# Two half quarters ahead of the first scores, a block sum split later, three gate buffers, a wait per block at the join, gate tiles ahead of weights

## What is computed

```
h = rms_norm(x, g_mix); z = h @ w_in
q, k, v, r, a_lr, c_b, c_c, c_x, g_a, g_b = split_columns(z)
o = gla_chunked(q, k, v, log_sigmoid(a_lr @ w_alpha_up + b_alpha) / 16)   # 4 heads, chunks of 64
o = rms_norm(o, g_gla) * silu(r)
y_a = o @ w_branch_a
y_b = (c_b * causal_dwconv(c_c * c_x, w_conv)) @ w_branch_b
x = x + (sigmoid(g_a) * y_a + sigmoid(g_b) * y_b) @ w_out
```

## Time and profile before

| | |
|---|---|
| time, median of 3 runs | 2441.77 us (2439.71 to 2442.86) |
| the profiled execution: its own time | 2438.01 us |
| its span, first to last instruction | 2436.4 us |
| PE busy | 2367.5 us (97%) |
| DVE busy | 1669.9 us (69%) |
| ACT busy | 1271.2 us (52%) |
| POOL busy | 384.8 us (16%) |
| mean granted TensorE clock | 0.989 of full speed |

### The profile page before, as it was taken

How to read it: one execution, slowest core, us unless ns; L and a number is a source line. 1 busy time by engine, 2 the same in 40 slices (tenths; PEclk the granted TensorE clock), 3 DMA queues, 4 the chain that set the end, 5 groups by cost and what they waited for, 6 DMA issues and landing times.

```text
span 2436.4 us, 40291 instructions
## 1 busy us (share of the span) xinstructions
PE 2367.5 (97%) x13303; PEld 1877.5 (77%) x13304; DVE 1669.9 (69%) x1750; ACT 1271.2 (52%) x1348; POOL 384.8 (16%) x412
## 2 busy tenths in 40 slices
PE   7999999999999999978999999999999999999996
PEld 7887777878887887876788777777777787777775
DVE  5212556757667264276789887888877998788977
ACT  5413653232223021165677665767666776667766
POOL 0000000000000001452121212122122121212120
PEclk9999999999999999998999999999999999999998
DMA  5133234353444333457999898989889998989998
GB/s 136 35 46 54 61 95 96 82 78 70 71 76 156 130 121 123 154 187 258 332 376 379 304 333 291 375 307 379 303 315 309 385 378 282 336 307 378 346 341 305
DMA packets 264906, 553.77 MB, mean 227 GB/s; under 512 B 29464, under 2 KB 76312, under 8 KB 263712
## 3 DMA queue, kind: packets, MB, share of 16 engines
q1 hardware_dynamic: 241536, 497.74, 61.0%
q0 software_dynamic: 23296, 55.03, 8.0%
HBM read 501.70 MB, written 51.02 MB: 227 GB/s over the span
## 4 chain that ended last, share of the span: by engine, by line
PE 53%; DVE 1%; issue 0%; ACT 0%; DMA 0%; POOLq 0%; DVEq 0%; ACTq 0%
PE m_y L2610 5%; PE m_gate L2612 5%; PE m_gate L2610 5%; PE m_lin L2610 5%; PE m_lin L2612 5%; PE m_gate L2611 5%; PE m_lin L2611 5%; PE m_y L2612 5%; PE m_y L2611 5%; PE m_spill L2649 4%; PE m_spill L2661 2%; PE m_turn L2594 1%; PE m_gate L2618 1%; PE m_y L2618 1%; PE m_lin L2618 1%; PE m_lin L2580 1%
## 5 line engine op out<-in xcount | busy, mean ns | idle before, releaser
L2418 DVE TENSOR_TENSOR m_w_lo<-raw,m_w_hi 128x2048 fp32r<-128x2048 f32 x382 | 867.1, 2288 | 204.4 <-ACT m_w_hi L2293 198.5
L2293 ACT CAST m_w_hi<-raw 128x2048 fp32r<-128x2048 f32 x382 | 730.9, 1914 | 351.3 <-PE m_lin L2612 236.8
L121 PE MATMUL c_bank<-h_hi_r,ring_hi 128*128 128x512 f32 x656 | 259.7, 396 | 3.4 <-DVE qk_r L1341 2.1
L2610 PE MATMUL m_gate<-m_w_hi,x_hi 128*128 128x512 f32 x508 | 216.2, 426 | 0.0
L2610 PE MATMUL m_y<-m_w_hi,m_a_hi 128*128 128x512 f32 x512 | 210.3, 411 | 1.8 <-DVE m_a_lo L2470 1.8
L2612 PE MATMUL m_y<-m_w_hi,m_a_lo 128*128 128x512 f32 x512 | 199.9, 390 | 0.0
L2611 PE MATMUL m_y<-m_w_lo,m_a_hi 128*128 128x512 f32 x512 | 199.8, 390 | 0.0
L2612 PE MATMUL m_gate<-m_w_hi,x_lo 128*128 128x512 f32 x508 | 199.2, 392 | 0.0
L2611 PE MATMUL m_gate<-m_w_lo,x_hi 128*128 128x512 f32 x508 | 198.6, 391 | 0.0
L2610 PE MATMUL m_lin<-m_w_hi,x_hi 128*128 128x512 f32 x508 | 198.6, 391 | 0.0
L2612 PE MATMUL m_lin<-m_w_hi,x_lo 128*128 128x512 f32 x508 | 198.3, 390 | 0.0
(11 more groups left out here) (416 smaller groups left out, 4675.2 us busy)
## 6 DMA issues: line engine op xcount, KB each, us to landing
raw<-in_w_gate_up SPq DMA_DIRECT2D x512, 512.0 KB, 11.1
raw<-in_w_down SPq DMA_DIRECT2D x256, 512.0 KB, 14.6
ring_raw<-in_w_in SPq DMA_DIRECT2D x31, 1024.0 KB, 9.6
gates<-work POOLq DMA_DIRECT2D x32, 256.0 KB, 3.8
work<-gates SPq DMA_DIRECT2D x8, 1024.0 KB, 7.2
v<-in_x SPq DMA_DIRECT2D x8, 512.0 KB, 6.0
r_rows<-work POOLq DMA_DIRECT2D x16, 256.0 KB, 2.8
o_rows<-v SPq DMA_DIRECT2D x8, 512.0 KB, 11.1
```

What stands on the lines that cost most here:

```text
L121: pe.matmul(out, left_hi(k), right_hi(k), start=first and k == kts[0], stop=False, skip_group_check=True)
L2293: act.copy(w_hi[:, p % WS].rearrange("p k b n -> p (k b n)"), raw[:, raw_slot(m)].rearrange("p k b n -> p (k b n)")).then_inc(signals.whi, 1)
L2418: dve.tensor_tensor(w_lo[:, p % WS].rearrange("p k b n -> p (k b n)"), raw[:, raw_slot(m)].rearrange("p k b n -> p (k b n)"), f32(w_hi[:, ...
L2610: pe.matmul(out, left_hi[:, kt], right_hi, start=False, stop=False, skip_group_check=True)
```

## The change

Five edits:

1. In the first attention tile, `gate_product(1, 0)` (12 matmuls) stands ahead of `score(0)` instead of between `update(0)` and `output(0)`.
2. ACT's `form_high(2)`, `form_high(3)` and `turned_hi(3)` stand ahead of the last `light_out` of the plain gate panels; DVE's `turned_lo(3)` moves from ahead of the seven-product loop to z = 0, f = 2.
3. A third gate buffer, and a semaphore for each buffer: `light_out(k)` waits for the store of quarter k-3. The new buffer lies over a buffer of the r gate, so quarter 2 also waits for the r gate's stores.
4. At the end of the projections PE waits before each of the four k blocks for that block's b_lo, not for all five b_lo at once.
5. In the join, SP loads the weights of panel A+1 only when silu tiles 5, 6 and 7 have landed.

```diff
@@ buffers
-        stream = take(2, HALF)
+        stream = [take(HALF), take(HALF)]
...
+        stream.append(take(HALF))
+        STREAMS = len(stream)
@@ stores
-        def gate_stores(k):
-            return 16 * (GATES // 2 + k // 2)
+        def stores(s, k=STREAMED):
+            return 16 * len(range(s, k, STREAMS))
@@ light_out, on ACT
-                if k >= 2:
-                    act.wait_ge(gate_stored[k % 2], gate_stores(k))
-                act.activation(stream[:, k % 2], value, ACT.Sigmoid).then_inc(light_done, 1)
+                if k >= STREAMS:
+                    act.wait_ge(stream_stored[k % STREAMS], stores(k % STREAMS, k))
+                if k == 2:
+                    for s in range(2):
+                        act.wait_ge(gate_stored[s], 16 * GATES // 2)
+                act.activation(stream[k % STREAMS], value, ACT.Sigmoid).then_inc(light_done, 1)
@@ plain gate panels, on ACT
                 act.wait_ge(ready, results(n) + r + 1)
+                if k == 4 * LIGHTS - 1:
+                    form_high(2)
+                    form_high(3)
+                    turned_hi(3)
                 light_out(k, banks[4 * (n % 2) + r][:, :])
...
-            form_high(2)
-            form_high(3)
-            turned_hi(3)
@@ DVE
             form_low(3)
-            turned_lo(3)
...
                     for at_m in forms_at(z, f):
                         form_low(at_m)
+                    if z == 0 and f == 2:
+                        turned_lo(3)
@@ PE, attention
             for i in range(TT):
                 gate_product(2 * i, 0)
+                if i == 0:
+                    gate_product(1, 0)
                 score(i)
                 gate_product(2 * i, 1)
                 update(i)
-                gate_product(2 * i + 1, 0)
+                if i:
+                    gate_product(2 * i + 1, 0)
                 output(i)
                 gate_product(2 * i + 1, 1)
@@ PE, end of the projections
-            pe.wait_ge(b_lo_done, HEADS + 1)
             pe.wait_ge(light_done, STREAMED)
             for k in range(HEADS):
+                pe.wait_ge(b_lo_done, k + 2)
                 for j in range(4):
                     channel_product(pe, ring, END, banks[j][:, :], b_hi, b_lo, j, kts=[k], first=k == 0, last=False)
@@ SP, join
                 sp.wait_ge(ready, results(n - 1))
+                if n == A + 1:
+                    for s in range(2, EARLY):
+                        sp.wait_ge(silu_loaded[s], 16)
```

More of the change, by code:

```diff
@@ L670, in attend_and_project @@
         gate_done, gate_stored = sem("gate_done"), signals.gate_stored
+        stream_stored = signals.stream_stored
         ready = sem("ready")
@@ L745, in _ @@
                 pool.wait_ge(light_done, k + 1)
-                pool.dma_start(gates[:, n * BPP + r // 2, (r % 2) * HALF:(r % 2 + 1) * HALF], stream[:, k % 2]) \
-                    .then_inc(gate_stored[k % 2], 16)
+                pool.dma_start(gates[:, n * BPP + r // 2, (r % 2) * HALF:(r % 2 + 1) * HALF], stream[k % STREAMS]) \
+                    .then_inc(stream_stored[k % STREAMS], 16)
             for s in range(2):
-                pool.wait_ge(gate_stored[s], gate_stores(STREAMED))
+                pool.wait_ge(gate_stored[s], 16 * GATES // 2)
+            for s in range(STREAMS):
+                pool.wait_ge(stream_stored[s], stores(s))
         @block.scalar
@@ L869, in _ @@
                     if z == SEVENS - 1 and f == 2:
-                        for s in range(2):
-                            act.wait_ge(gate_stored[s], gate_stores(STREAMED))
+                        for s in range(STREAMS):
+                            act.wait_ge(stream_stored[s], stores(s))
                         act.copy(b_hi(HEADS), qk[:, HEADS]).then_inc(b_hi_done, 1)
@@ L2007, in __init__ @@
         self.gate_stored = [sem(f"gate_stored{s}") for s in range(2)]
+        self.stream_stored = [sem(f"stream_stored{s}") for s in range(3)]
         self.added = [sem(f"added{x}") for x in range(2)]
```

## The result

The changed kernel takes 2428.0 us (median of 5 runs, 2424.68 to 2432.04), beside 2441.77 for the kernel before (5 runs, 2439.71 to 2448.45): a ratio of 0.9941, with a 95% interval of 0.9921 to 0.9961. It is faster by 0.6%, or 13.8 us in the medians; 10.5 were forecast, for a time of 2431.3. The profiled execution took 2432.04 us with a span of 2430.4, the slowest of the five.

What follows compares the result with a forecast made beforehand. PE, busy 97% of the span, bounds the kernel, so only its gaps and slow clock can give: 4.5 + 1.2 + 1.3 + 2.4 + 1.1 = 10.5 us off 2441.8 gives 2431.3 us, range 2427.5 to 2436.0.

Steps and rivals of the forecast that it cites:

- no stall for the states: First attention tile: DVE's states stay 0.2 us ahead of the outputs; stall costed at nothing, 0.5 us at most.
- The rival, that the clock falls in tile 0 all the same: First attention tile: PE's clock still falls, gain 8.8 us instead of 10.5, time 2433.0 us; chance 0.11.
- The barrier's 0.3 us of room: Join's barrier: DVE's last split ends at 783.49, 0.3 us before PE now arrives at 783.8; it barely fits.
- the part on the clock: Attention stage: clock 0.50 behind the 3.04 us gap, full speed behind shorter ones; filling it gains 4.5 us, otherwise 2.85.
- the 3.8 us by which the profiled execution lay under the median: Whole kernel: profiled execution took 2438.0 us, 3.8 under the median; 10.5 was subtracted from the median 2441.8.
- The router rival: Router stage: 12 us more PE work at the lower clock gives back 6 us, time 2437.3 us; chance 0.11.
- a sign of being wrong: Listed signs: new gaps before first outputs, product 5 of z = 0, the barrier or panel A+1; or a longer router stage.
- The weights of A+1: Panel A+1: held weights land 6.2 us late at worst loads, gain falls to 3.2 us, time 2438.6; slower-case chance 0.03.

Runs made afterwards that it cites:

- before, second: The kernel before plus a register operation holding the expert stage's loaded routed-row counts at zero or above: 2439.64 us (11 runs), 0.9999 to the original.
- before, third: The kernel before with the same register operation on the expert stage's counts, run once more: 2442.07 us in one run.
- after, second: The changed kernel plus a register operation holding the expert stage's loaded counts at zero or above, against the kernel before with it: 2429.22 us (6 runs), 0.9954.
- after, third: The changed kernel with the same register operation, timed once more against the kernel before: 2426.74 us (5 runs), 0.9944.
- the second series: Both kernels again, each with only a register operation on the expert stage's counts added: before 2439.64 us, changed 2429.22 us, ratio 0.9954.
- The two kernels built on the change: The changed kernel with panel A's last two tiles' transposes moved ahead (2428.28 us, 0.9935 to before), and with the join's single b_lo wait restored (2434.21 us, 0.9958).

## Why the prediction was right, and where it fell short

The stretch piece by piece, in three profiles of each kernel (each figure the difference of two starts on PE: first scores, fourth product of z = 0, that of z = 5, first product behind the join's barrier, first of the output stage; the total begins at the stage's start, 6.0 us ahead of the scores):

| profile | scores to z = 0 | to z = 5 | to the barrier | to the output stage | total |
|---|---|---|---|---|---|
| before | 208.09 | 97.87 | 253.76 | 175.50 | 741.24 |
| before, second | 208.12 | 97.90 | 259.06 | 175.11 | 746.21 |
| before, third | 208.13 | 97.94 | 256.79 | 175.15 | 744.05 |
| after | 202.72 | 96.28 | 250.93 | 174.31 | 730.27 |
| after, second | 202.71 | 96.39 | 251.41 | 174.33 | 730.87 |
| after, third | 202.72 | 96.40 | 253.56 | 174.32 | 733.03 |
| forecast gain | 5.7 | 1.3 | 2.4 | 1.1 | 10.5 |
| mean gain | 5.4 | 1.5 | 4.6 | 0.9 | 12.4 |

- **Edit 1**, 4.5 counted, 4.3 measured alone (208.09 - 203.78). Scores at the old time, full clock behind them, no stall for the states: all as said. The rival, that the clock falls in tile 0 all the same, is refuted in each of the seven profiles that have the whole or half block ahead. The Trainium skill ("TensorE: Matmul & The Clock Gate", section "What's actually happening") has the throttled state as the default that activity releases; the trace agrees, since filling 2.7 of the 3.04 us kept the clock at 1.00.
- **Edit 2**, 1.2 counted, 1.1 measured. `turned_lo(3)` stood from 432.63 to 434.9 and held up no product.
- **Edit 3**, 1.3 counted, 1.5 measured up to z = 5: that gap went to 0.69 to 1.03 where 1.0 was said. The reason given, that quarter 15 still waits for the store of quarter 12, is what the trace shows. What the sum did not have is z = 12, which stands behind gate panel z = 11 as z = 5 stands behind z = 4, and had no gap in the one profile that I read. In the eight profiles with two buffers it is 0.93 us on average, from nothing to 1.93; in the six with three buffers 0.50, from nothing to 2.33. It hangs on a store's landing in both, and with this scatter no gain there is shown.
- **Edit 4**, 2.4 counted, 2.5 measured alone. From z = 5 to the barrier the changed kernel against the one with three buffers alone gives the same, 253.46 - 250.93 = 2.5. The barrier's 0.3 us of room held: the split ends at 777.65 and the product starts at 778.18, with the same 0.30 before it as ever.
- **Edit 5**, 1.1 counted, 0.8 to 1.2 measured. Silu tiles 5 to 7 loaded in 3.8 to 5.5 us in all six profiles with this edit, no wait of DVE for a silu tile in panel A, and DVE bound by PE's transposes as said, which moving them ahead then proved. The rule of the Trainium skill weighed for it ("DMA: Bandwidth & Descriptors", section "Queues, rings and completion order"), that an engine takes packets in turn from its queues, agrees for the silus: without the weights beside them the last one lands in 5.3 us and not in 10.3. Its other use, that a third store does not slow the two ahead of it, agrees too: the store of quarter 12 (gate panel z = 4) landed after 11.6, 11.6 and 11.5 us in the three profiles of before and after 11.5, 11.7 and 11.7 in those of after, and the one behind it after 9.6 to 9.8 in all six.

The fixed parts measured add up to 4.3 + 1.1 + 1.5 + 2.5 + 0.9 = 10.3 us, 10.5 counted. **The step that failed** is the one in the part on the clock, that "the first matmuls behind the gaps of 1.36, 1.87 and 2.23 us are drawn at 0.47 to 0.50 us, as at full speed", read as if the clock did not fall behind these gaps, so that each was priced at its length and 0.16. For the profile that it was read from this was true: the clock was 1.00 behind each of these gaps. But the first matmul says little of it, as in the falls behind such gaps the clock went down 0.1 to 1.3 us behind the gap (an estimate from the mean clock of each microsecond), and one execution without a fall is not a kernel without one. In the second and third profile of before the clock fell twice and once behind such gaps: three falls of 1.6 us in three executions, 1.6 a time on average. Over all profiles that have these gaps it is 5 of 9, 2 of 8, 3 of 8 and, at z = 12, 1 of 8: 1.3 falls an execution, an estimate of 2.1 us. That is the difference between 10.3 and the mean gain of 12.4, or most of it (in the table it stands in "to the barrier": 4.6 for 2.4); the rest is scatter, since at z = 12 the two means are equal to 0.1 us. A kernel that closes such gaps gains their length and the falls that come with some of them.

The same step hides in the 3.8 us by which the profiled execution lay under the median. The forecast kept them and took from the median only what this one execution could lose. The other two profiled executions of before, at 2442.73 and 2442.07 us, had 5.0 and 2.8 us more in the changed stretch: stalls and falls that the change removes in part.

How much of the 13.8 us is this step and how much chance, the times do not say. The three ratios, 0.9941, 0.9954 and 0.9944, lie around both readings: 12.4 us of 2441 is 0.9949, 10.5 us is 0.9957, the first interval reaches from 0.9921 to 0.9961, and the second series has its medians 10.4 us apart. What the profiles show is the stretch.

**The router rival** (6 us given back) did not come in full, but it is not nothing. From the output stage to the end before took 1474.4, 1474.3 and 1475.6 us, after 1477.9, 1477.9 and 1475.1: 2.2 more on average. It lies in the router stage, where a longer time was named as a sign of being wrong: from the output stage's first product to the first of the experts it takes 143.4, 143.5 and 144.2 us before, and 147.7, 147.1 and 144.0 after, 2.6 more on average. That first product of the experts, before and after in the first two profiles:

```profile
1105.39 0.61 PE L2618 MATMUL m_gate<-b_split,m_pick 128*128 128x512 bf16 x1 [2.01 <-DVE m_pick L2424]
```

```profile
1100.20 0.63 PE L2635 MATMUL m_lin<-b_split,m_pick 128*128 128x512 bf16 x1 [2.41 <-DVE m_pick L2441]
```

The two kernels built on the change take 145.5 and 145.3 there, the six with one edit or a part of one 142.3 to 145.3. So some 2 us seem to be given back, but the ranges touch, and what would do it stays open. Ahead of the attention stage, where no instruction changed, it is 220.8, 220.6 and 220.8 against 222.2, 223.6 and 221.0, 1.5 more. That looks like chance: the six kernels with one edit or a part of one have anything from 219.6 to 223.4 there. The two together are why the profiled spans differ by 8.7 us on average and not by 12.4. Whether the timed runs lose it too stays open: each of the three profiled executions of the changed kernel was the slowest of its series (2432.04, 2433.91 and 2430.66 beside medians of 2428.0, 2429.22 and 2426.74), as was the second one of before (2442.73), and there is no trace of the others.

The weights of A+1 were never late; that rival fell.

## What to carry to other kernels

A gap of TensorE near two microseconds should be priced at its length, and at a share of a fall of the clock besides; look at the granted clock of the microseconds behind the gap, not at the first matmul alone. Read more than one profile of the kernel before where a gap hangs on a DMA's landing: a stall that one execution does not show can be the largest of the next. An edit of one microsecond is seen between two landmarks on the bounding engine (the scores to z = 0 in the changed kernel: 202.72, 202.71 and 202.72 us in three executions), where the total time scatters by several.

## What the hardware showed that was not expected

- Behind gaps of 1.7 to 2.4 us in the changed stretch PE's clock went to the level of 1.2 GHz (0.50) in some executions and stayed at 2.4 GHz in others, at the same place of the same program. Over all profiles: 5 of 9 behind the join's gap of 2.23 to 2.25 us, 2 of 8 behind that at z = 5 (1.77 to 2.00), 3 of 8 in panel A (1.69 to 2.13), 1 of 2 at z = 12 (1.93, but not 2.33), none behind the 1.68 before the scores. Behind the gap of 3.04 it fell in all seven profiles that have it, in three of them while PE still waited; behind the one of 1.36 and all shorter ones in none. A longer gap is thus no sure sign of a fall: 2.33 went by without one, and so did the 1.78 at the entry to the output stage in all fourteen profiles. What decides it between executions no run here shows. The section of the Trainium skill named above says of the start of a kernel that the number of slow matmuls differs between runs of one kernel; here the same is seen in its middle.
- A store of 256 KB landed in 2.3 us at best and in 12.2 at worst, with other stores and the weights' load of a panel in flight beside it. How far it moves with the execution depends on the place: in ten profiles the store of quarter 12 took 11.5 to 11.8 us, that of the first quarter of gate panel z = 11 took 8.6 to 12.2.
